# A two-layer transformer block: residual stream by tokens, norms and routing overlapped with products, first expert item in front of the loop, additions of scaled outputs on GpSimd

## What is computed

```
x  = x + gt1 * rmsnorm(merge(o_a, o_b, ...) @ w_o, g_post_mix)
h2 = rmsnorm(x, g_pre_ffn) * (1 + sc2) + sh2
logits = h2 @ w_router + b_router ; top 4 of 32, softmax over the four
f  = sum over the chosen experts of weight * (swiglu(h2 @ w_gu[e] + b_gu[e]) @ w_dn[e] + b_dn[e])
x  = x + gt2 * rmsnorm(f, g_post_ffn)
h  = rmsnorm(x, norm_mix)        ; GLA and Fox on h @ w_in, gates, w_out
x  = x + y @ w_out
x  = x + (gelu(conv(a)) * val) @ w_down   with a, val = rmsnorm(x, norm_ffn) @ w_up
out = rmsnorm(x, norm_final)
```

## Time and profile before

| what | value |
|---|---|
| runs of the kernel | 1844.46, 1847.75, 1848.31 us; median 1847.75 us |
| the profiled execution | 1846.86 us, its span 1844.7 us |
| TensorE busy | 1714.3 us, 93% of the span |
| VectorE, ScalarE, GpSimd busy | 424.3 us (23%), 253.7 us (14%), 9.6 us (1%) |
| DMA | 538.5 MB, mean 292 GB/s, some 428 GB/s inside the loop over the experts |
| idle before L715, up to its release | 554.6 us in 33 items: ScalarE waits for TensorE |

### The profile page before, as it was taken

One profiled execution on the slowest core, in us unless ns is written; L12 is line 12 of the kernel. 1 busy time (PEld: TensorE's weight loads), 2 busy tenths in 40 slices (PEclk: granted clock), 3 DMA queues, 4 the chain that ended last, 5 costly groups with the idle time before them and its releaser, 6 DMA issues.

```text
span 1844.7 us, 20627 instructions
## 1 busy us (share of the span) xinstructions
PE 1714.3 (93%) x8428; PEld 944.4 (51%) x8428; DVE 424.3 (23%) x962; ACT 253.7 (14%) x491; POOL 9.6 (1%) x6
## 2 busy tenths in 40 slices
PE   4999999599999999999999999999979999899998
PEld 2766678433333333333333333333354688788887
DVE  2303331412112111111211111121131623244401
ACT  2013330201001010000101000010131220011000
POOL 0010000000000000000000000000000000000000
PEclk9999999799999999999999999999989999999999
DMA  9553620679999999999999999999943232344300
GB/s 396 206 137 131 280 92 9 273 278 431 427 428 430 427 430 428 429 430 427 429 429 428 428 428 429 429 427 430 428 192 150 92 137 91 137 147 173 137 23 23
DMA packets 49465, 538.52 MB, mean 292 GB/s; under 512 B 15856, under 2 KB 16048, under 8 KB 16656
## 3 DMA queue, kind: packets, MB, share of 16 engines
q1 hardware_dynamic: 37152, 533.74, 69.3%
q10 hardware_dynamic: 12272, 4.19, 1.2%
HBM read 536.86 MB, written 1.05 MB: 292 GB/s over the span
## 4 chain that ended last, share of the span: by engine, by line
PE 59%; DMA 35%; DVE 3%; ACT 1%; issue 1%; SPq 0%; ACTq 0%; DVEq 0%
DMA ring<-experts_dram 35%; PE scores L1652 11%; PE proj L1363 9%; PE proj L1855 8%; PE proj L1371 6%; PE proj L1866 4%; PE proj L1488 3%; PE att_out L1675 3%; PE proj L1537 3%; PE scores L1332 2%; PE proj L1407 1%; PE scores L1453 1%; PE turned L1611 1%; PE att_out L1477 1%; DMA rows<-rows_dram 1%; PE proj L1504 1%
## 5 line engine op out<-in xcount | busy, mean ns | idle before, releaser
L1652 PE MATMUL scores<-ring,arena 128*64 128x512 f32 x2112 | 475.3, 594 | 34.4 <-DMA ring<-experts_dram 30.9
L1652 PEld LDWEIGHTS scores<-ring,arena 128*64 128x64 f32 x2112 | 147.5, 137 | 350.5 <-issue 262.7
L1675 PE MATMUL att_out<-ring,arena 128*64 128x512 f32 x1056 | 241.2, 598 | 0.0
L1363 PE MATMUL proj<-arena,ring 128*128 128x256 f32 x768 | 169.9, 382 | 2.6 <-DVE arena L994 2.6
L1855 PE MATMUL proj<-arena,ring 128*128 128x256 f32 x704 | 154.5, 383 | 5.7 <-DVE arena L1161 5.7
L1363 PEld LDWEIGHTS proj<-arena,ring 128*128 128x128 f32 x768 | 145.9, 191 | 25.1 <-DVE arena L994 3.4
L1855 PEld LDWEIGHTS proj<-arena,ring 128*128 128x128 f32 x704 | 135.3, 192 | 24.9 <-DVE arena L1161 6.1
L1675 PEld LDWEIGHTS att_out<-ring,arena 128*64 128x64 f32 x1056 | 70.1, 136 | 145.3 <-issue 118.5
L1136 DVE COPY arena<-turned 128x512 f32<-128x512 f32 x33 | 22.8, 692 | 504.2 <-PE turned L1611 504.2
L1371 PE MATMUL proj<-ring,arena 128*128 128x512 f32 x256 | 111.1, 593 | 0.0
L715 ACT ACTIVATE arena<-att_out 128x512 f32<-128x512 f32 x33 | 19.7, 598 | 554.6 <-PE att_out L1616 554.6
(11 more groups left out here) (299 smaller groups left out, 1142.1 us busy)
## 6 DMA issues: line engine op xcount, KB each, us to landing
ring<-experts_dram SPq DMA_DIRECT2D x198, 2048.0 KB, 24.1
ring<-stream_dram SPq DMA_DIRECT2D x54, 2048.0 KB, 7.8
ring<-stream_dram SPq DMA_DIRECT2D x2, 1024.0 KB, 17.8
arena<-rpb_dram ACTq DMA_DIRECT2D x16, 128.0 KB, 4.4
xT<-xT_dram SPq DMA_DIRECT2D x1, 1024.0 KB, 6.9
arena<-ctxT_dram SPq DMA_DIRECT2D x1, 1024.0 KB, 9.5
out_dram<-arena SPq DMA_DIRECT2D x2, 512.0 KB, 2.6
...
```

What stands on the lines that cost most here:

```text
L1363: ins = mm(pb[:, c * T:c * T + T], W[:, k, (c0 + c) * P:(c0 + c) * P + P], src[:, k, :], start=k == 0, stop=k == K - 1)
L1652: ins = mm(AS[n][parts, :], xe[:, k % 4, k // 4, :], W[:, kk, n * D + feats.start:n * D + feats.stop], start=False, stop=k == KD - 1, skip ...
L1675: ins = mm(AO[parts, :], act_s[:, kk, s - 4, :], W[:, kk, feats], start=s == 4 and kk == 0, stop=s == 5 and kk == 3)
```

## The change

The residual stream is kept by tokens after attention: `xtok` is 128 tokens by 2 tiles by 1024. A second copy of x is read for it at the head. The parts:

- w_o, w_out and the down product of the FFN are made with tokens stationary, tile by tile and in halves of 512 columns. Squares come from ScalarE with a running sum along the row, so mean, root and reciprocal are one column each (`square_half`, `token_mean`, `token_root`, `token_rstd`), and the products with ones are gone. Gains along columns are needed as rows spread over the partitions: VectorE scales the modulation rows in attention, ScalarE writes them to DRAM and reads them back (`gain1`, `gain2`).
- VectorE writes y times rstd times gain to `scaled`, GpSimd adds it to `xtok`: eight additions of 128 x 512, four after w_o and four after the experts. The additions after w_out and down stay on VectorE.
- The router works on the turned x itself: its weights are multiplied by A2 beforehand (`wr2`), the shift's part is one row (`crow`), the token's rstd comes in with the logits. The gather takes `xtok` with `Sel` times rstd, and the factor and the shift are put on `xe` by two VectorE passes (`expert_input`) in place of ScalarE's copy.
- Item 0 stands in front of the loop (`expert_item(0, first=True)`); the table of items, the overflow and the down biases are worked out inside it. SyncE issues expert 1's reads without the table, and the loops begin at 1 and 2.
- After the experts and after w_out, the normed halves are turned by TensorE (`turn_normed`). In layer 2 the v projection is taken first, tile 0 before tile 1. The output is written in four pieces.

```diff
+            for s in range(RING):
+                sp.wait_ge(up_slot, RING + s + 1)
+                expert(slice(1, 2), s)
+            sp.wait_ge(route_dve, 5)
             n_items = sp.value_load(table[0:1, ITEMS:ITEMS + 1], min_val=NE, max_val=ITEMS - 1)
-            with sp.Fori(1, n_items) as i:
+            with sp.Fori(2, n_items) as i:
...
+            pool.wait_ge(xtok_in, 16)
+            for c in range(8):
+                tt, h = c // 2 % TT, c % 2
+                pool.wait_ge(y_scaled, c + 1)
+                x_ = xtok[:, tt, half_of(h)]
+                nc.gpsimd.tensor_tensor(x_, x_, scaled[:, h, :], ALU.add).then_inc(x_half, 1)
...
+                if w == 7:
+                    act.wait_ge(rows_scaled, 1)
+                    for j in range(2):
+                        act.dma_start(mod_dram[0:1, half_of(j)], modrow[32 * j:32 * j + 1, :]).then_inc(rows_out, 16)
+                if w == 9:
+                    act.wait_ge(rows_out, 32)
+                    act.dma_start(gain1, mod_dram[0, :].partition_broadcast(P)).then_inc(gain1_in, 16)
...
+            load_table(ACT.Sqrt)
+            squares_of_y(0)
+            token_root(0)
+            square_of_x(0)
+            square_of_x(1)
+            token_root(1)
+            copy_x_turned(0)
+            copy_x_turned(1)
+            squares_of_y(1)
+            token_root(2)
+            square_of_x(2)
+            copy_x_turned(2)
+            square_of_x(3)
+            token_root(3)
+            load_table(ACT.Exp)
+            act.wait_ge(top_ready, 1)
...
+                V.tensor_tensor(wr2, wr[:], bc(A2, NE, mid=False), ALU.mult)
+                step(V.tensor_tensor(wr3, wr[:], bc(mod[:, 24:32, 0], NE, mid=False), ALU.mult))
+                V.reduce_sum(prodc, wr3.rearrange("p k e -> p e k"), AX.X).then_inc(router_scaled, 1)
...
-            scale_banks(yT, M1 + 8, 3, 2 + 4)
-            add_to_x(yT, lambda k: gt1[:, k:k + 1])
-            dve.wait_ge(x_mid, KD)
-            dve.wait_ge(root_ready, 4)
-            step(V.reciprocal(rstd, rstd))
-            for k in range(KD):
-                V.scalar_tensor_tensor(out=sqy[:, k, :], in0=xT[:, k, :], scalar=A2[:, k:k + 1], in1=rstd,
-                                       op0=ALU.mult, op1=ALU.mult).then_inc(scaled_ready, 1)
...
+            def scale_y(c, n, gain):
+                tt, h = c // 2 % TT, c % 2
+                if c % 4 >= 2:
+                    dve.wait_ge(x_half, c - 1)
+                V.scalar_tensor_tensor(out=scaled[:, h, :], in0=PB[2 * tt + h][:, :], scalar=tok_r[:, n:n + 1],
+                                       in1=gain[:, half_of(h)], op0=ALU.mult, op1=ALU.mult).then_inc(y_scaled, 1)
...
+            def expert_input(one_step):
+                one_step(V.tensor_tensor(xe, AO[:, :].rearrange("p (a h c) -> p a h c", h=2, c=CAP),
+                                         A2.rearrange("p (h a) -> p a h", a=4).unsqueeze(3)
+                                         .to_broadcast([P, 4, 2, CAP]), ALU.mult))
+                V.tensor_tensor(xe, xe, mod[:, 24:32, 0].rearrange("p (h a) -> p a h", a=4).unsqueeze(3)
+                                .to_broadcast([P, 4, 2, CAP]), ALU.add).then_inc(xe_ready, 1)
...
+                dve.wait_ge(xg_t, i + 2)
+                expert_input(mstep)
...
-            norm_x(6, "norm_mix")
...
+            def norm_half(hn, tt, h, n, gain):
+                V.scalar_tensor_tensor(out=hn[:, tt, half_of(h)], in0=xtok[:, tt, half_of(h)], scalar=tok_r[:, n:n + 1],
+                                       in1=gain[:, half_of(h)], op0=ALU.mult, op1=ALU.mult).then_inc(hn_ready, 1)
...
-            for n in range(2):
-                need(23 + n)
-                for b in range(2):
-                    features(slot(23 + n, KD, 512), mergedT, 2 * b)
-            sum_squares(sqy, AS[0], 3)
-            sum_squares(sqy, AS[0], 4)
...
+            need(23)
+            tokens(slot(23, KD, 512), mergedT, 0)
+            need(24)
+            tokens(slot(24, KD, 512), mergedT, 0)
+            tokens(slot(23, KD, 512), mergedT, 1)
+            turn_x(0)
+            turn_x(1)
+            tokens(slot(24, KD, 512), mergedT, 1)
+            router(0)
+            turn_x(2)
+            turn_x(3)
+            router(1)
...
-            def combine():
-                for k in (0, 4, 1, 5, 2, 6, 3, 7):
-                    half = slice(CAP * (k // 4), CAP * (k // 4) + CAP)
-                    ins = mm(sum_at(k), yb[half, (k % 4) * P:(k % 4) * P + P], SelWT[half, :],
-                             start=False, stop=False, skip_group_check=True)
+            def combine(tt):
+                for h in range(2):
+                    rows_ = slice(CAP * h, CAP * h + CAP)
+                    ins = mm(PB[2 * tt + h][:, :], SelWT[rows_, tile_of(tt)], yb[rows_, :], start=False, stop=False,
+                             skip_group_check=True)
...
+                    if first and s == 0:
+                        overflow_counts()
+                    if first and s == 1:
+                        overflow_columns()
...
+            turn_normed(hn1, 0, 0)
+            turn_normed(hn1, 1, 0)
+            pe.wait_ge(hT_ready, 2)
+            need(0)
+            tokens(slot(0, KD, 512), hT, 0)
+            turn_normed(hn1, 2, 0)
+            turn_normed(hn1, 3, 0)
+            pe.wait_ge(hT_ready, 4)
...
+            tokens(slot(0, KD, 512), hT, 1)
...
-                need(12 + n)
-                for b in range(2):
-                    features(slot(12 + n, KD, 512), merged2, 2 * b)
-            sum_squares(sq2, AS[0], 7)
-            pe.wait_ge(h_ready, 4 * KD)
+            need(12)
+            need(13)
+            for tt in range(TT):
+                for h in range(2):
+                    tokens(slot(12 + h, KD, 512), merged2, tt)
+            for c in range(4):
+                turn_normed(hn2, c, 4)
+            pe.wait_ge(hT_ready, 8)
...
-            pe.wait_ge(dve_evac2, KD + 4 + 22)
-            for n in range(6):
-                need(DN0 + n)
-                pe.wait_ge(actT_ready, min(2 * n + 2, 11))
-                K = shape2[DN0 + n][0]
-                W = slot(DN0 + n, K, D)
-                for j in range(KD):
+            for c in range(4):
+                tt, h = c // 2, c % 2
+                pe.wait_ge(dve_evac2, KD + 18 + c + 1)
+                for n in range(6):
+                    if c == 0:
+                        need(DN0 + n)
+                        pe.wait_ge(actT_ready, min(2 * n + 2, 11))
+                    K = shape2[DN0 + n][0]
                     for k in range(K):
-                        ins = mm(PB[j // 2][:, (j % 2) * T:(j % 2) * T + T], W[:, k, j * P:j * P + P],
-                                 actT[:, 4 * n + k, :], start=n == 0 and k == 0 and j % 2 == 0, stop=n == 5 and k == K - 1,
-                                 skip_group_check=True)
-                    if n == 5 and j % 2:
-                        ins.then_inc(down_slots, 1)
-                if n < 5:
-                    ins.then_inc(down_slots, 1)
-            sum_squares(sq2, AS[0], 8)
+                        ins = mm(PB[c][:, :], actT[:, 4 * n + k, tile_of(tt)], slot(DN0 + n, K, D)[:, k, half_of(h)],
+                                 start=n == 0 and k == 0, stop=n == 5 and k == K - 1)
+                ins.then_inc(down_done, 1)
```

705 lines of the change are left out of this document (422 added, 283 removed).

## The result

The changed kernel takes 1804.76 us (median of 4 runs, 1804.37 to 1806.05), the kernel before 1846.39 us in the same comparison (4 runs, 1844.46 to 1848.31). The ratio is 0.9776, 95% interval 0.9759 to 0.9793. The forecast was 1801 us, 1793 to 1812. The profiled execution of the changed kernel took 1806.05 us with a span of 1804.2, so 40.8 us (40.5 of span) are to be found against the 46.7 of the sum.

The account below looks back on a forecast made before the run. TensorE (59% of the chain) and DMA (35%) bound the kernel, the weight stream setting the loop's end. 26.1 - 0.5 - 0.1 + 10.5 + 2.4 + 2.7 + 5.6 = 46.7 off 1846.86 gave 1800.2, plus 0.9 for the median: 1801 (1793 to 1812).

Parts of the forecast that it names:

- Step 1: Routing and stream start: item 0 near 344.5 instead of 378.62, the weight stream never pauses; gain 26.1 us, 0.5 charged.
- step 6: Attention: VectorE's extra work comes 1.1 us late but is covered, ScalarE's new issues fall into its waits; 0 us taken.
- The bound for the pause, 0 to 4: Start of the expert loop: range in us for a short pause of the weight stream, charged at 0.5.
- 26.1 - 0.5: Expert loop: gain in us from the earlier weight stream, less the charge for a short pause.
- The rival of a pausing stream: Expert loop start: routing takes 28 us instead of 19, item 0 frees slots 5 to 9 us late; 1808, chance 0.12.
- Step 2: One expert item: two VectorE passes on xe leave TensorE under 29.36 us; only the last item shows 0.1 us.
- the cover: Expert loop: 1.8 us by which TensorE's item can grow before it passes the stream's 29.36 us.
- every microsecond costs 33: Expert loop: price in us of each microsecond an item grows beyond the 1.8 us that TensorE has to spare.
- Step 3: After the experts: last combination to layer 2's first projection 12 us, clock cost 3 taken; gain 10.5 us, range 7 to 13.
- Steps 4 and 5: FFN norm: gain 2.0 plus 0.4 us; down's start and form: 2.0 and 0.7; the end: 5.6.
- slowed by VectorE: GpSimd additions: each takes 2.2 us instead of 1.1 beside VectorE's passes; 1806, chance 0.17.
- Slower than before: Expert loop: an item grows past the stream, slower than before from 3.2 us, 1874 at 4 us; chance 0.03.

Follow-up runs that it names:

- e1: Changed kernel with ScalarE's six small reads for layer 2 (two w_in_2, four alpha_w2) issued early, in w_o's time: 1795.66 us, ratio 0.9731.
- e12: The same kernel as e1, run once more in a later group: 1796.55 us, ratio 0.9734.
- e6: e1 with two more VectorE passes on xe in each expert item: 1797.33 us, one run.
- e7: e1 with four more VectorE passes on xe in each expert item: 1860.21 us, one run.
- e3: Changed kernel with the eight additions to xtok on VectorE, right behind each scaling, instead of on GpSimd: 1807.44 us, ratio 0.979.

## Why the prediction was right, and where it wasn't

**Forecast and result.** 1801 was 3.8 us below 1804.76; it lay in the range, and on the right side. Against the profiled execution the sum missed more, 5.9 us (1800.2 and 1806.05). That the medians are closer comes from 0.8 added for the median of before and from the profiled execution lying 1.3 above the median of its group: that part is luck. The mechanism that carried the forecast, the stream's start, is confirmed by e1: without the hold, the stream ran through from 324.1 on without a gap, and the last up slot came at 1282.6 (1285.4 in e12), against 1286 in the prediction. Had e1 been the changed kernel, the forecast would have been 5.3 too high.

**Step 1, the failed step.** "The stream never pauses", with 0.5 charged, and in step 6 "ScalarE's new DMA issues fall into its waits, since it is busy for 14% of the span". By the prediction's own sign ("a pause of the stream after 356 ... would prove it wrong") this step was wrong, though the time lay in the range. What came before it was right: w_o's end at 324.33 (325.1), routing 19.2 us (19), item 0 at 343.5 (344.5). Inside the 19, terms made up for each other: the router's products took 3.03 instead of 2 and the gather 3.68 instead of 3.0, both at a granted clock of 0.50 to 0.58, and the short operations and hand-overs took less than was charged. What failed is that six issues that already existed weren't looked at when the work around them moved. In the kernel before they stood behind the routing as well, but the stream stood still there (issued 377.9 to 380.6, landed in 1.9 to 2.6 us for `alpha_w2`). By moving the stream's running time over them the change made the third of them last 36.5 us. The prediction's own point, that the stream would run without a gap from w_o's end, was the condition for it. The bound for the pause, 0 to 4, was too narrow for the same reason. Of the terms, 26.1 - 0.5 measured 18.2; without the hold it measures 29.5 in e1 and 26.8 in e12. One term was put too long, and so the gain too small: item 0's six reads at 31.1 us, as a stretch by itself, while in e1 the slots come at 4.89 each from w_o's end on, 29.3 for six. With w_o's end, 1.0 earlier than predicted, that is 2.8 of the 3.4 us by which e1's last up slot comes before 1286. One more sign failed even without the hold: the first wait for the ring was expected in item 1 or 2, and the chain of e1 has its first DMA piece at 523.25, in item 6. The stream sets the end of the loop, but the first items run at TensorE's pace on slots that were read ahead.

**The rival of a pausing stream** gave 1808 with 0.12, because routing might take 28 us. The pause came, 8.7 us and in its size as foreseen, but not from there. A time near a rival's doesn't make its mechanism right.

**Step 2.** The down products start 2.41 us behind the last activation pass, as in the earlier trace rows: 1304.86 and 1307.27. Nothing per item. e6 confirms the cover; e7 shows that "every microsecond costs 33" beyond it is too low, since the waiting TensorE also loses clock.

**Step 3.** 12.6 us to the first projection (12 predicted), which took 9.74, 2.9 more than the 6.87 at full speed (3 predicted): its granted clock was 0.50 until 1332, 0.61 to 1334, and 1.00 from there. From the start of the combination to the end of the token projection it was 72.0 before (1333.85 to 1405.90) and 60.7 after: 11.3 against 10.5.

**Steps 4 and 5.** 6.8 (7.2), no gap in front of down, 6.3 at the end (6.6): each within half a microsecond, because each was a list of operations with durations from rows of the same form.

**GpSimd.** Its addition took 1.25 us, estimated at 1.1 from an instruction of 4096 columns. The rival "slowed by VectorE" (2.2 each) was wrong in direction: the additions took 2.48 to 2.51 for two wherever they stood, and VectorE's short operations were stretched instead, by 0.5 to 0.6 each. The Trainium skill's GPSIMD Engine Reference (3.1, and 8, Key points) speaks for VectorE here. Its ratio of speeds is borne out in kind, 1.25 to 0.69, and its contention is seen, but nothing speaks for following the advice here: e3 isn't faster, and its trace is 1.2 us slower from the last up slot to the first projection. On this chain of scale, add, square, two engines side by side beat one that is faster.

**Slower than before** (0.03) would have needed an item past the stream; e7 shows how it would have looked, 64.6 us on top of e1 for 2.8 us an item.
